# Both swiglus: blocks 4 to 11 of the second projection as seven products of quarters instead of eight

## The chip, the core and the metric

The kernel runs on one core of a Trainium2 chip. The metric is the device time of one execution in microseconds (us); TensorE is called PE here, VectorE DVE, ScalarE ACT, GpSimd POOL and SyncE SP. Before the change the median of three runs is 1713.47 us (1713.27 to 1714.15).

## The reference, cut to what matters

Two transformer layers and a third block of another kind run one after the other on 512 tokens of 1024 features, all in float32. The change touches the feed-forward part of the two layers, which stands after an attention and a layer norm in each:

```python
D_FF = 2816
def swiglu(x, w_in, w_out):
    gate, up = jnp.split(x @ w_in, 2, axis=-1)
    return (jax.nn.silu(gate) * up) @ w_out
x = layer_norm(DEEPNORM_ALPHA * x + swiglu(x, ffn_w_in[l], ffn_w_out[l]), ln_g[l, 1], ln_b[l, 1])   # l = 0, 1
```

The hidden activations have 2816 features, which are 22 blocks of 128. The third block ends in a feed-forward part too (`square(relu(f)) @ w_ff2`, 32 blocks), and its second projection is already computed in the way that the change brings to the swiglus.

## The kernel before, in words

**Numbers.** Each float32 operand is split into a high part, rounded to the type that PE multiplies (ACT writes it, `whi`, `hh`, `xh`), and the rest (DVE writes it, `wlo`, `hl`, `xl`). A product of two matrices then takes three matmuls (`mm3`).

**The swiglu stage.** `ffn` first computes blocks 0 to 3 plainly (`projections`). Blocks 4 to 21 are made by `pairs`: gate and up of one block form a pair, and their first projection is seven `product` steps of 12 matmuls of 256 columns each, with sums of the two weight tiles on DVE (`sums`, four instructions), copies out of PSUM on ACT (`keep`), sums on DVE (`combine`, `hidden`), silu on ACT (`gates`), and at last the hidden block (`hidden`), its high part on ACT and its low part on DVE (`hidden_low`).

**The second projection.** `rows` multiplies hidden blocks by rows of `ffn_w_out`, in groups of blocks (`FFN_GROUPS`: 4, 4, 4, 2, then 8 at the end). One piece is six matmuls of 512 columns: 128 tokens, two blocks, 512 output columns. Four blocks take 16 pieces, 4 split weight tiles and 8 additions from PSUM into `x` on DVE.

**The order.** All engines run through one list of steps (`Plan.steps`), each engine in that order and in order only. `PIECES` has a word of four digits for each iteration of `pairs`: how many pieces stand at four places between the products of that iteration. A split weight tile is a unit; `pump` puts its split so many units ahead of its use (`AHEAD_PAIRS` = 3). Eight slots hold split tiles.

**The seven products, as the last block has them.** For four hidden blocks at a time, `seven` takes the tokens, the hidden blocks and the output columns in halves and forms seven products of sums of quarters (`SEVEN`: a11, a12, s1, s4, s2, s3, a22), two pieces for each. `left_sum` forms the sums of hidden quarters on DVE, `left` splits each of the seven left operands (high part ACT, low part DVE), and the right operands are weight tiles to which an accumulating DMA from POOL's queue adds further tiles. A product is added to the output after each piece: nine of the 14 by DVE (`fadd`), five by ACT into `low_words` and then by an accumulating DMA from POOL's queue (`moved`, semaphores `added`). The raw hidden blocks lie in `hidden_words`, in the same memory as `hh`; `low_words` lies in the memory of `hl`.

Of the kernel before, what the change touches and what calls it, by code (L numbers as in the profile page):

```python
# [31 lines left out]
PIECES = "1011 1011 1011 1011 1011 1111 1111 1111 1111 1111 1111 1111 1111 1011 0101 0101 0101 0101 0000".split()  # L32
# [4 lines left out]
SEVEN_FIRST, SEVEN_LAST = 1, 6  # L37
# [8 lines left out]
PIECES = "1011 1011 1011 1011 1011 1111 1111 1111 1111 1111 1111 1111 1111 1011 0101 0101 0101 0101 0000".split()  # L46
# [27 lines left out]

class Piece:


    def __init__(self, u, unit, t, bank, start, before, value, tile, nh, sign, sent, earlier, after):
        self.u, self.unit, self.t, self.bank, self.start, self.before, self.value = u, unit, t, bank, start, before, value
        self.tile, self.nh, self.sign, self.sent, self.earlier, self.after = tile, nh, sign, sent, earlier, after  # L80
        self.moved = moved(tile, nh)


class Right:


    def __init__(self, buffer, need, sums=(), load=None):
# [3 lines left out]
class Pair:  # L91
# [8 lines left out]
    def __init__(self, kind, n, table, columns, blocks, first=None):  # L100
# [3 lines left out]
        self.first, self.seven = first, None if first is None or first // 4 > SEVEN_LAST else first // 4  # L104
# [35 lines left out]
class Plan:  # L140


    def __init__(self, kinds=None):
        self.steps, self.tiles, self.finished = [], [], {}
        self.units, self.kinds, self.summed = [], kinds, 0
# [8 lines left out]
        self.entry_of, self.entry_free = {}, {}  # L154
# [51 lines left out]
    def pump(self, most=2):  # L206

        while most and self.kinds and self.n_split < min(len(self.units) + self.ahead, len(self.kinds)):
# [7 lines left out]
            self.free_at.append(free)  # L216
            if SPLIT <= slot < SPLIT + EXTRA:
# [6 lines left out]
    def sum_next(self):  # L224

        n = self.n_split
        if n > self.summed and n < len(self.kinds) and self.kinds[n] == "s2":
            for i in range(3):
                self.prepare("sums", n + i)
            self.summed = n + 2  # L230
# [123 lines left out]
    def rows(self, kind, source, row0, nk, k_first=0, hh=True, norm=None, group=0):  # L354
# [14 lines left out]
        for word in order:  # L369
# [30 lines left out]
            if last:  # L400
                self.release(r.bank)
                self.step("rows_post", r)
                if kind == "f" and group == 0:
                    self.plain_rows = r.value
            self.relax(PACE[0])
# [117 lines left out]
    def seven(self, g):  # L523

        def ring(n):
            k = SEVEN_FIRST + n // 3
            return None if k > SEVEN_LAST else (n % 2 + 2, (4 * k + (2, 2, 0)[n % 3], (0, 1, 1)[n % 3]))

        first, last = 4 * g, 4 * g + 2
        turn, a = g - SEVEN_FIRST, g % 2  # L530
        needs = []
        for n in range(3):
            r = 3 * (g - SEVEN_FIRST) + n
# [3 lines left out]
        following = (a, (4 * g + 8, 0)) if g + 2 <= SEVEN_LAST else None  # L537
        landed = turn // 2 * 16 + 16
        rights = [Right(a, ("load", landed), [(a, "a", (first, 1))]), Right(b, ("load", b_need), (), b_next),
                  Right(a, ("a", 48 * turn + 16), [(a, "a", (last, 1))]),  # L540
                  Right(c, ("load", c_need), [(d, "d", (last, 1))], c_next),
                  Right(a, ("a", 48 * turn + 32), [(a, "a", (last, 0))]), Right(d, ("d", 16 * turn + 16), (), d_next),
                  Right(a, ("a", 48 * turn + 48), (), following)]
        rights[3].before = d_need
        if g == SEVEN_FIRST:
            self.paced = True
            self.left(1)
        for n, (name, chain, start, m, nh, sign) in enumerate(SEVEN):
            u = 7 * (g - SEVEN_FIRST) + n
            unit = self.unit("seven", rights[n], None)  # L550
            if g == SEVEN_LAST and n == 6:
                self.step("gain", self.fifth)
                self.step("unpark", unit)
            for t in range(2):
                if (chain, t) not in self.chains:
# [4 lines left out]
                piece = Piece(u, unit, t, bank, start, self.evicts.get(bank), value, tile, nh, sign, sent,  # L560
                              self.added.get((tile, nh)), after)
# [6 lines left out]
                if g == SEVEN_LAST and n == (3 if chain else 6):  # L568
                    self.release(bank)
                self.step("seven_post", piece)  # L570
                self.relax(PACE[0])
                if t == 1:
                    self.left(u + 2)
                self.flush()
                yield

# [7 lines left out]
    def left(self, u):  # L584

        g, n = SEVEN_FIRST + u // 7, u % 7
        if g > SEVEN_LAST:
# [13 lines left out]
        entry = (2, 3, 0, 1)[u % 4] if g < SEVEN_LAST else 2 + u % 2  # L601
# [13 lines left out]
    def product(self, pair, j):  # L615
# [24 lines left out]
        if j in (2, 7, 3):  # L640
            pair.combined[j] = self.count("combined") + 1
            self.read[{2: (1, 0), 7: (7, 0), 3: (6, pair.buf)}[j]] = pair.combined[j]
            if j != 3 and pair.kind == "relu":
                self.step("combine", pair, j, pair.clear)
            elif j != 3:
# [2119 lines left out]
```

## Time and profile before

| | |
|---|---|
| median of three runs | 1713.47 us |
| the profiled execution | 1713.66 us, its span 1711.9 us, granted PE clock 0.999 |
| matmuls | 10386 |
| PE busy | 1697.1 us |
| DVE busy | 1243.1 us |
| swiglu pairs | about 300 to 550 us and 900 to 1150 us of the span |
| seven products of the last block | about 1460 to 1670 us |

PE's busy time counts a matmul until its modelled end, so that it overlaps the next. The time that a matmul takes from the engine is the distance of two starts. The profiled execution lies 0.19 us above the median, and 1.8 us of it lie outside the span.

### The profile page before, as it was taken

To read this page: it belongs to the slowest core of one execution; us is meant where nothing else is said; L and a number is where in the kernel's file an instruction comes from. 1 tells how busy PE (TensorE), PEld (TensorE's weight loads), DVE (VectorE), ACT (ScalarE), POOL (GpSimd) and SP (SyncE) were. 2 spreads that over 40 slices of the span, in tenths; PEclk is the share of its full clock that TensorE was granted. 3 is DMA by queue.
4 is the path that set the end of the run, shared out by engine and by line. 5 is a ranking of instruction groups with operands and counts; after the bars stand their busy time and mean duration, and the time that the engine had idled before them with its cause. 6 is when DMAs were issued, how large, how long until landed. Compare 5 with 4: busy or idle time off the path is not lost.

```text
span 1711.9 us, 26482 instructions
## 1 busy us (share of the span) xinstructions
PE 1697.1 (99%) x10386; PEld 1480.7 (86%) x10386; DVE 1243.1 (73%) x2019; ACT 881.9 (52%) x1559; POOL 92.7 (5%) x157
## 2 busy tenths in 40 slices
PE   9999999999999999999999999999999999999998
PEld 7777788999999897777989999998988899899997
DVE  4588887777787745665877777868536686998897
ACT  4477744444444234665344444443546465766664
POOL 0222000000000000000000000000000000122121
PEclk9999999999999999999999999999999999999999
DMA  7343332333234332222233323343222335788875
GB/s 276 115 136 119 113 99 87 111 100 103 95 101 135 122 99 87 78 83 88 73 111 111 91 95 111 99 162 98 90 73 86 111 111 160 181 201 189 197 164 153
DMA packets 64559, 206.03 MB, mean 120 GB/s; under 512 B 8833, under 2 KB 9762, under 8 KB 64434
## 3 DMA queue, kind: packets, MB, share of 16 engines
q1 hardware_dynamic: 54610, 179.68, 32.5%
q0 software_dynamic: 9824, 24.65, 8.0%
q8 instruction: 83, 1.36, 0.3%
q14 instruction: 42, 0.34, 0.1%
HBM read 188.00 MB, written 9.48 MB: 115 GB/s over the span
## 4 chain that ended last, share of the span: by engine, by line
PE 94%; DVE 4%; ACT 1%; DMA 1%; issue 0%; SPq 0%; POOL 0%; DVEq 0%; ACTq 0%
PE ps L904 29%; PE ps L905 28%; PE ps L906 28%; PE ps L1319 1%; PE ps L1364 1%; PE ps L1390 1%; PE ps L1339 1%; PE ps L1378 1%; PE ps L1197 1%; DVE wlo L1965 0%; PE ps L1329 0%; DVE xl L2093 0%; DMA arena<-in_c_xt 0%; DVE small L2161 0%; DVE x L2157 0%
## 5 line engine op out<-in xcount | busy, mean ns | idle before, releaser
L1965 DVE TENSOR_TENSOR wlo<-raw,whi 128x1024 fp32r<-128x1024 f32 (+1 forms) x252 | 289.1, 1162 | 126.1 <-ACT whi L1551 125.8
L904 PE MATMUL ps<-xh,whi 128*128 128x256 f32 (+1 forms) x1016 | 331.7, 326 | 2.3 <-DVE xl L2093 2.3
L906 PE MATMUL ps<-xh,wlo 128*128 128x256 f32 (+1 forms) x1016 | 325.5, 320 | 0.0
L905 PE MATMUL ps<-xl,whi 128*128 128x256 f32 (+1 forms) x1016 | 325.2, 320 | 0.0
L1551 ACT ACTIVATE whi<-raw 128x1024 fp32r<-128x1024 f32 (+1 forms) x252 | 250.0, 1004 | 44.8 <-PE ps L906 27.6
L906 PE MATMUL ps<-whi,hl 128*128 128x512 f32 x604 | 235.4, 390 | 0.0
L904 PEld LDWEIGHTS ps<-xh,whi 128*128 128x128 f32 x1016 | 193.4, 190 | 25.9 <-issue 8.8
L904 PE MATMUL ps<-whi,hh 128*128 128x512 f32 x536 | 213.4, 398 | 0.7 <-DVE wlo L1965 0.6
L905 PE MATMUL ps<-wlo,hh 128*128 128x512 f32 x536 | 209.9, 392 | 0.0
L906 PEld LDWEIGHTS ps<-xh,wlo 128*128 128x128 f32 x1016 | 193.4, 190 | 14.4
L905 PEld LDWEIGHTS ps<-xl,whi 128*128 128x128 f32 x1016 | 193.6, 191 | 12.2
L904 PE MATMUL ps<-t_of,whi 128*128 128x256 f32 x624 | 176.0, 282 | 0.9 <-ACT stat L1559 0.9
L906 PE MATMUL ps<-t_of,wlo 128*128 128x256 f32 x624 | 176.6, 283 | 0.0
L905 PE MATMUL ps<-t_of,whi 128*128 128x256 f32 x624 | 176.5, 283 | 0.0
L906 PEld LDWEIGHTS ps<-whi,hl 128*128 128x128 f32 x604 | 113.4, 188 | 25.0
L904 PEld LDWEIGHTS ps<-t_of,whi 128*128 128x128 f32 x624 | 119.2, 191 | 7.2 <-ACT stat L1559 1.4
L905 PEld LDWEIGHTS ps<-t_of,whi 128*128 128x128 f32 x624 | 119.2, 191 | 5.3
L906 PEld LDWEIGHTS ps<-t_of,wlo 128*128 128x128 f32 x624 | 119.2, 191 | 0.0
L904 PEld LDWEIGHTS ps<-whi,hh 128*128 128x128 f32 x536 | 101.1, 189 | 20.6 <-issue 1.8
L904 PE MATMUL ps<-whi,xh 128*128 128x512 f32 x292 | 116.1, 398 | 1.0 <-DVE wlo L1923 0.6
L905 PEld LDWEIGHTS ps<-wlo,hh 128*128 128x128 f32 x536 | 101.1, 189 | 16.4 <-issue 0.2
L905 PE MATMUL ps<-wlo,xh 128*128 128x512 f32 x292 | 114.1, 391 | 0.0
(299 smaller groups left out, 3276.3 us busy)
## 6 DMA issues: line engine op xcount, KB each, us to landing
raw<-in_c_tiles SPq DMA_DIRECT2D x263, 512.0 KB, 3.7
x<-in_c_row_tiles SPq DMA_DIRECT2D x24, 512.0 KB, 5.6
x<-in_c_row_tiles POOLq DMA_DIRECT2D x24, 512.0 KB, 5.9
arena<-low_words POOLq DMA_DIRECT2D x30, 256.0 KB, 5.9
bias_skewed<-bias_rows SPq DMA_DIRECT2D x8, 640.0 KB
arena<-arena POOLq DMA_DIRECT2D x64, 64.0 KB, 3.5
arena<-bias_skewed SPq DMA_DIRECT2D x16, 256.0 KB, 4.1
x<-in_x SPq DMA_DIRECT2D x4, 512.0 KB, 5.8
```

What stands on the lines that cost most here:

```text
L904: e.matmul(o, ah, bh, start=start, stop=False, **more)
L905: e.matmul(o, ah, bl, start=False, stop=False, **more)
L906: return e.matmul(o, al, bh, start=False, stop=stop, **more)
L1197: m = e.transpose(ps[b][:, k * 128:k * 128 + 128], src[:, c:c + 128], ident[:])
L1319: e.matmul(ps[b][:, 0:n], q[c, i * 128:i * 128 + 128], k[c, 0:n], start=True, stop=True).then_inc(s.scores, 1)
L1339: m = e.matmul(ps[b][:, j * 128:512], self.V[:, j, h * 128:h * 128 + 128], self.aT[:, j, j * 128:512], start=(j == 0), stop=(j == 3))
L1364: m = e.matmul(ps[b][:, 0:n], q[c, queries], k[c, 0:n], start=turn == 0, stop=turn == 2)
L1378: m = e.transpose(ps[b][:, j * 128:j * 128 + 128], e_[:, j * 128:j * 128 + 128], ident[:])
L1390: m = e.matmul(ps[b][64 * a:64 * a + 64, j * 128:512], self.V_b[:, j, h * 64:h * 64 + 64], self.PT[a][:, j, j * 128:512], start=(j == 0), ...
L1551: e.activation(self.parts(m)[0][:, 0:n], src, ACT.Copy).then_inc(s.hi, 1)
L1965: e.tensor_tensor(lo[:, 0:n], src, f32(hi[:, 0:n]), ALU.subtract).then_inc(s.lo, 1)
```

## The change: what it does, and the diff

In both swiglus, hidden blocks 4 to 11 (groups 1 and 2) go through `seven` instead of `rows`; groups 0, 3 and 4 stay plain. The hidden product of these blocks is written raw to `hidden_words` and has no low part of its own. `seven`, `left` and their helpers take a `Stage`. The sums of products go to `x`. The right operands lie in the arena where two extra slots of split tiles were; these are closed at iteration 2 of `pairs` and opened again after it, and two small slots take the 512-column unit of each pair. `PIECES` has four pieces in each of the iterations 6 to 12; splits and sums are put off one by one (`SWIGLU_PACE`). The low parts of blocks 12 to 15 are written to the memory of `hl` that the moved products of group 1 pass through, and so wait for its accumulating DMAs; those of blocks 16 to 19 wait for group 2's.

```diff
-PIECES = "1011 1011 1011 1011 1011 1111 1111 1111 1111 1111 1111 1111 1111 1011 0101 0101 0101 0101 0000".split()
+PIECES = "1011 1011 1011 1011 1011 0010 1111 1111 1111 1111 1111 1111 1111 1101 0101 0101 0001 0000 0000".split()
+SWIGLU_AHEAD = 4
+CLOSE_AT, LOADS_FROM = 2, 3
+SWIGLU_PACE = 1, 1
+LEFT_AT = 5
+STAGES = [Stage(0, "ffn_w_out0", 1, 2, 0), Stage(1, "ffn_w_out1", 1, 2, 2), Stage(2, "w_ff2_2", 1, 6, 4)]
...
+        self.after = stage.base + stage.groups - (first % 8 >= 4) if first < 4 * stage.last + 12 else 0
...
 def pairs(self, pairs, pieces, places, ahead, first=(0, 0)):
         for i in range(len(pairs) + 1):
+            if i == LEFT_AT and self.stage.n < 2:
+                self.left(self.stage, 0)
+                self.left(self.stage, 1)
+            if i == CLOSE_AT and self.loads:
+                self.close_extra()
+            if i >= LOADS_FROM and self.loads:
+                self.step(*self.loads.pop(0))
...
-        rows = [self.rows("res", (f"ffn_w_out{layer}", 0), f0, nf, norm=norm if f0 == 14 else None, group=g)
+        rows = [self.seven(stage, g) if stage.covers(g) else
+                self.rows("res", (f"ffn_w_out{layer}", 0), f0, nf, norm=norm if f0 == 14 else None, group=g)
                 for g, (f0, nf) in enumerate(FFN_GROUPS)]
...
             elif what == "hidden":
+                elif pair.seven is not None:
+                    w.wait_ge(s.gates, pair.gates)
+                    w.wait_ge(self.events[free[0]], free[1])
+                    e.tensor_tensor(self.hidden_words[:, pair.blocks[0], :], first, second, ALU.mult).then_inc(s.combined, 1)
...
             elif what == "hidden_low":
                 for i, k in enumerate(pair.blocks):
-                    if pair.kind == "relu":
-                        for n in range(MOVED * (SEVEN_LAST - SEVEN_FIRST) - 4, MOVED * (SEVEN_LAST - SEVEN_FIRST)):
+                    if pair.after:
+                        for n in range(MOVED * pair.after - 4, MOVED * pair.after):
                             w.wait_ge(s.added[n % 4], 16 * (n // 4 + 1))
                     w.wait_ge(s.hh, pair.hidden[i] + 1)
                     e.tensor_tensor(self.hl[:, k, :], self.pair_out[pair.kind][i][pair.buf], f32(self.hh[:, k, :]),
```

**DVE, around the low part of block 12.** DVE's queue before, in the ninth of the 18 pairs of the first swiglu: the sum and the product that make the hidden block, a 512-column split of a weight tile, the low part of block 12 (it waits for its high part alone), the next split and the sums of the next pair.

```order
L2036 TENSOR_TENSOR arena<-arena,ps 128x256 [waits s_product]
L2047 TENSOR_TENSOR arena<-arena 128x512 [waits s_gates,s_combined]
L1965 TENSOR_TENSOR wlo<-raw,whi 128x512 [waits s_hi]
L2056 TENSOR_TENSOR hl<-arena,hh 128x512 [waits s_hh]
L1965 TENSOR_TENSOR wlo<-raw,whi 128x1024 [waits s_hi]
L1998 TENSOR_TENSOR arena<-stat,ps 128x256 [waits s_product,s_copied]
```

The same place in the changed kernel, from the same two rows on. L2103 is the low part of a left operand, L2134 the low part of block 12, L2039 a split, L2097 the addition of a product to `x`, L2082 a sum of hidden quarters.

```order
L2110 TENSOR_TENSOR arena<-arena,ps 128x256 [waits s_product]
L2125 TENSOR_TENSOR arena<-arena 128x512 [waits s_gates,s_combined]
L2059 TENSOR_TENSOR raw<-raw,arena 128x512 [waits s_sums,s_lo]
L2062 TENSOR_TENSOR raw<-raw 128x512
L2103 TENSOR_TENSOR xl<-hidden_words,xh 128x2x256 [waits s_left_hi]
L2134 TENSOR_TENSOR hl<-arena,hh 128x512 [waits s_added0,s_added3,s_hh,s_added2,s_added1]
L2039 TENSOR_TENSOR wlo<-arena,whi 128x1024 [waits s_hi]
L2039 TENSOR_TENSOR small_slots<-raw,small_slots 128x512 [waits s_hi]
L2097 TENSOR_TENSOR x<-x,ps 128x512 [waits s_rows]
```

The low part of block 12 now waits for the four semaphores of the accumulating DMAs, and splits, additions to `x` and sums stand behind it.

**DVE, a little further on.** Seven rows after the last of those stands this stretch: a split, the sums of the next pair, its hidden block, an addition to `x`, and the sums s2 and s4 of hidden quarters (L2084, L2086) with a left operand.

```order
L2039 TENSOR_TENSOR wlo<-arena,whi 128x1024 [waits s_hi]
L2053 TENSOR_TENSOR arena<-raw 128x512 [waits s_raw2,s_raw3,s_lo,s_sums]
L2055 TENSOR_TENSOR arena<-arena,raw 128x512 [waits s_sums]
L2110 TENSOR_TENSOR arena<-arena,ps 128x256 [waits s_product]
L2125 TENSOR_TENSOR arena<-arena 128x512 [waits s_gates,s_combined]
L2059 TENSOR_TENSOR raw<-raw,arena 128x512 [waits s_sums,s_lo]
L2097 TENSOR_TENSOR x<-x,ps 128x512 [waits s_fadd,s_rows]
L2062 TENSOR_TENSOR raw<-raw 128x512
L2084 SCALAR_TENSOR_TENSOR arena<-arena,hidden_words 128x512 [waits s_left_sum]
L2086 SCALAR_TENSOR_TENSOR hidden_words<-hidden_words,arena 128x2x256 [waits s_left_sum]
L2103 TENSOR_TENSOR xl<-hidden_words,xh 128x2x256 [waits s_left_hi]
L2134 TENSOR_TENSOR hl<-arena,hh 128x512 [waits s_hh]
```

The sixth row behind these is the split of the right operand of product s4 of group 2 (an L2039 row of 1024 columns). From the waiting low part to that split, both counted, there are 31 rows on DVE: 8 of 1024 columns, 19 of 512 and 4 of 256; before, a pair's rows were followed by those of the next pair and by the splits and additions of plain pieces alone.

**POOL.** Before, nothing of POOL's queue stood in the swiglus. Now the first group of seven has these rows (L2564 adds a weight tile to a right operand, L2573 adds a moved product to `x`), the last of which is the product that block 12's low part waits for:

```order
L2564 DMA arena<-in_c_row_tiles 128x1024 [waits s_lo] x2
L2564 DMA arena<-in_c_row_tiles 128x1024 [waits s_right2]
L2573 DMA x<-low_words 128x512 [waits s_res,s_evicted]
L2564 DMA arena<-in_c_row_tiles 128x1024 [waits s_lo]
L2573 DMA x<-low_words 128x512 [waits s_evicted]
L2573 DMA x<-low_words 128x512 [waits s_added1,s_evicted]
L2573 DMA x<-low_words 128x512 [waits s_added0,s_evicted]
L2564 DMA arena<-in_c_row_tiles 128x1024 [waits s_lo]
L2573 DMA x<-low_words 128x512 [waits s_evicted]
```

The last L2564 row serves group 2 already. So a group brings nine transfers of POOL's queue, four of 512 KB and five of 256 KB, where there were none.

## Rows read from the trace of the kernel before

**Rows 1.** The page: busy time of each engine, and the chain that ended last.

```profile
PE 1697.1 (99%) x10386; PEld 1480.7 (86%) x10386; DVE 1243.1 (73%) x2019; ACT 881.9 (52%) x1559; POOL 92.7 (5%) x157
...
PE 94%; DVE 4%; ACT 1%; DMA 1%; issue 0%; SPq 0%; POOL 0%; DVEq 0%; ACTq 0%
```

**Rows 2.** Windows: the swiglu's pairs (two windows), seven products of the last block.

```profile
core 0: us, PE busy (x) PEld busy (x) DVE busy (x) ACT busy (x) POOL busy (x), PEclk, DMA share, GB/s
...
342.40:385.20 42.80, 42.80 (x299) 39.96 (x298) 30.80 (x42) 19.47 (x32) 0.00 (x0) 1.00 0.33 100
...
470.80:513.60 42.80, 42.80 (x308) 40.45 (x308) 35.53 (x51) 19.60 (x33) 0.00 (x0) 1.00 0.35 101
...
1540.80:1583.60 42.80, 42.80 (x271) 38.70 (x271) 38.56 (x53) 28.36 (x46) 8.68 (x10) 1.00 0.83 190
```

**Rows 3.** PE's waits, 260 to 560 us: total, times, longest.

```profile
PE ps L904 <- ACT stat L1559: 0.5, 1, 0.5
PE ps L904 <- DVE wlo L1965: 0.3, 1, 0.3
```

**Rows 4.** Timeline, last block: a piece's last matmuls, product, moved product's way.

```profile
1611.13 0.40 PE L904 MATMUL ps<-whi,hl 128*128 128x512 f32 x1
1611.37 0.39 PE L905 MATMUL ps<-wlo,hl 128*128 128x512 f32 x1
1611.60 0.39 PE L906 MATMUL ps<-whi,hl 128*128 128x512 f32 x1
...
1611.82 0.28 PE L904 MATMUL ps<-t_of,whi 128*128 128x256 f32 x1
1611.94 0.28 PE L905 MATMUL ps<-t_of,whi 128*128 128x256 f32 x1
1612.02 0.60 ACT L1586 ACTIVATE low_words<-ps 128x512 f32<-128x512 f32 x1
...
1612.93 0.86 POOL L2491 DMA_DIRECT2D arena<-low_words  x1 [4.00 <-ACT low_words L1586]
```

**Rows 5.** Accumulating DMAs of `low_words`, issue to landing: that at 1612.93, all 21.

```profile
DMA to landing us min/median/max: 4.8/4.8/4.8
...
DMA to landing us min/median/max: 3.3/6.2/7.6
```

**Rows 6.** DVE's timeline in the last block (start, duration, idle time before it).

```profile
1560.72 0.41 DVE L1998 TENSOR_TENSOR arena<-stat,ps 128x256 f32<-128x256 f32 x1
1561.05 0.41 DVE L1998 TENSOR_TENSOR arena<-arena,ps 128x256 f32<-128x256 f32 x1
...
1570.13 0.68 DVE L1979 TENSOR_TENSOR arena<-raw 128x512 f32<-128x512 f32 x1
1570.85 0.69 DVE L1981 TENSOR_TENSOR arena<-arena,raw 128x512 f32<-128x512 f32 x1
1571.64 0.69 DVE L1985 TENSOR_TENSOR raw<-raw,arena 128x512 f32<-128x512 f32 x1
1572.26 0.68 DVE L1988 TENSOR_TENSOR raw<-raw 128x512 f32<-128x512 f32 x1
1572.86 1.22 DVE L1965 TENSOR_TENSOR wlo<-arena,whi 128x1024 fp32r<-128x1024 f32 x1
...
1579.34 0.68 DVE L2008 TENSOR_TENSOR arena<-hidden_words 128x512 f32<-128x512 f32 x1
1580.72 0.69 DVE L2029 TENSOR_TENSOR hl<-arena,hl 128x512 fp32r<-128x512 f32 x1 [0.70 <-ACT hl L1579]
1581.33 0.68 DVE L2023 TENSOR_TENSOR arena<-arena,ps 128x512 f32<-128x512 f32 x1
1581.93 1.22 DVE L1965 TENSOR_TENSOR wlo<-x,whi 128x1024 fp32r<-128x1024 f32 x1
1583.06 0.68 DVE L2023 TENSOR_TENSOR arena<-arena,ps 128x512 f32<-128x512 f32 x1
```

**Rows 7.** Groups of instructions by line, 342.4 to 470.8 us: count, busy us, mean ns.

```profile
L1610 ACT ACTIVATE hh<-arena 128x512 fp32r<-128x512 f32 x9 | 5.7, 632 | 27.0 <-DVE arena L2047 27.0
```

More of the change, by code:

```diff
@@ L72, in moved, with __init__, covers @@
     return tile % 2 == 1 and (tile, nh) != (1, 0)
+class Stage:
+    def __init__(self, n, table, first, last, base):
+        self.n, self.table, self.first, self.last, self.base = n, table, first, last, base
+        self.groups = last - first + 1
+    def covers(self, group):
+        return self.first <= group <= self.last
+STAGES = [Stage(0, "ffn_w_out0", 1, 2, 0), Stage(1, "ffn_w_out1", 1, 2, 2), Stage(2, "w_ff2_2", 1, 6, 4)]
 class Piece:
-    def __init__(self, u, unit, t, bank, start, before, value, tile, nh, sign, sent, earlier, after):
+    def __init__(self, stage, u, unit, t, bank, start, before, value, tile, nh, sign, sent, earlier, after, last, summed):
+        self.stage, self.last, self.summed = stage, last, summed
         self.u, self.unit, self.t, self.bank, self.start, self.before, self.value = u, unit, t, bank, start, before, value
@@ L582, in with_last, with left @@
                 yield
-    def left(self, u):
-        g, n = SEVEN_FIRST + u // 7, u % 7
-        if g > SEVEN_LAST:
+    def left(self, stage, at):
+        g, n, u = stage.first + at // 7, at % 7, 7 * stage.base + at
+        if g > stage.last:
             return
@@ L653, in product @@
             pair.gates = self.count("gates") + 1
[L654 removed]
+            self.step("gates", pair, pair.clear)
         if j == 3:
@@ L717, in ffn @@
         name = f"ffn_w_in{layer}"
-        self.pairs([Pair("swiglu", f, name, (FF + f * 128, f * 128), [f % 8]) for f in range(PLAIN, 22)], pieces, PIECES,
-                   AHEAD_PAIRS)
+        self.pairs([Pair("swiglu", f, name, (FF + f * 128, f * 128), [f % 8], f, stage) for f in range(PLAIN, 22)],
+                   pieces, PIECES, SWIGLU_AHEAD)
         assert next(pieces, None) is None
+        self.small = None
+        self.open_extra("rows", self.counts["rows"])
         self.ffn_blocks[layer] = self.counts["h"]
@@ L973 @@
 MOVED = 5
-FADD = (14 - MOVED) * (SEVEN_LAST - SEVEN_FIRST + 1)
+FADD = (14 - MOVED) * sum(stage.groups for stage in STAGES)
 LAST = len(FEED_GROUPS) - 1
@@ L2037, in vector @@
                                 ALU.add).then_inc(s.combined, 1)
-                if pair.seven is not None:
+                if pair.seven is not None and pair.kind == "relu":
                     continue
@@ L2156, in vector @@
                     w.wait_ge(s.x, 64)
+                    if r.added is not None and moved(t, nh):
+                        w.wait_ge(s.added[r.added % 4], 16 * (r.added // 4 + 1))
+                    elif r.added is not None:
+                        w.wait_ge(s.fadd, r.added)
                     e.scalar_tensor_tensor(x[:, t, c], x[:, t, c], 1.0 if r.group else ALPHA, ps[b][:],
```

211 lines of the change are left out of this document (127 added, 84 removed).

## The prediction

> **What bounds the kernel now.** I read the page first, then windows, then PE's waits, then single rows. The page has PE busy for 99% of the span, and 94% of the chain that ended last is PE's [rows 1]. Busy time alone doesn't prove that PE has no slack, so I looked at the swiglu's pairs: in both windows PE is busy for all of 42.80 us, DVE for 30.8 and 35.5 us and ACT for less than 20 [rows 2], and in 300 us around the first swiglu PE waits 0.8 us in all [rows 3]. So PE's own work sets the time there, matmul by matmul. What is to be seen beside it: in the last block's stretch of seven products PE is just as full, but DVE is at 38.6 of 42.8 us and the DMA engines at 0.83, against 0.33 to 0.35 in the swiglu [rows 2]. The form that the change brings is thus known to run without stalls, but close to DVE's limit, and there with seven pieces to a pair of blocks' products, not four.
>
> **What is removed.** A group of four blocks takes 16 pieces before and 14 after. Two groups in two swiglus: 8 pieces, 48 matmuls of 512 columns less (9476 rows of PE become 9428). Successive starts of such matmuls lie 0.23 us apart [rows 4]: 1611.13, 1611.37, 1611.60, and the next kind at 1611.82. A piece is 6 x 0.23 = 1.38 us. The gain is 48 x 0.23 = 11.0 us, 5.5 us in each swiglu, all of it on the path as long as PE stays full.
>
> **What is added, in DVE's time.** DVE's costs are distances of starts [rows 6]: 1024 columns 1.13 us (1581.93 to 1583.06), 512 columns 0.60 (1581.33 to 1581.93), 256 columns 0.33 (1560.72 to 1561.05). The four sums of a pair take 2.73 together (1570.13 to 1572.86), since two of them wait for the one before. A left operand behind a sum has to go to ACT and back: DVE idles 0.70 us (the row at 1580.72).
> - A plain group costs DVE four splits, eight additions and four low parts: 4 x 1.13 + 12 x 0.60 = 11.7 us.
> - A group of seven costs seven splits, nine additions, seven left low parts and four left sums: 7 x 1.13 + 20 x 0.60 = 19.9 us, and three of those 0.70 us of idling, 22.0.
> - A pair costs three splits of 1024, one of 512, the sums, three combinations and the hidden product: 3.4 + 0.6 + 2.7 + 1.0 + 0.7 = 8.4 us, 9.0 with a low part.
>
> PE's time for an iteration with four pieces: a product is 12 matmuls 0.12 us apart (1611.82, 1611.94 [rows 4]), 1.44 us; seven products and four pieces are 10.1 + 5.5 = 15.6 us. The 28 pieces of seven fill seven iterations, 109 us of PE. DVE has 7 x 9.0 less two low parts, and two groups: 61.8 + 44.0 = 106 us. Before, seven such iterations cost it about 63 + 1.75 x 11.7 less the low parts counted twice (4.2) = 79 us. So DVE goes from 73% to 97% in that stretch: it just fits if nothing stops it, and has 3 us to catch up in.
>
> **The wait that stops it.** DVE's row of block 12's low part waits for all accumulating DMAs of group 1, and it stands right behind that group's last piece (a22, moved). Its cover is gone by construction, so I price the whole path from the end of that piece's last matmul on PE. In the last block, eviction starts 0.20 us after it (1611.82 to 1612.02), lasts 0.60, and POOL's transfer starts 1.11 us after PE's end (1612.93) [rows 4]; this very kind, the last of a group, landed after 4.8 us [rows 5]. That makes 5.9 us. In the swiglu ACT first has to make the high part of block 12, which waits for DVE's product of the same pair: 0.6 us more [rows 7]. I take **6.5 us** from the end of the piece until DVE goes on. The ends are 3.3 us of landing and no copy ahead (4.4 us) and 7.6 us of landing with it (9.3) [rows 5]. What is queued behind it on DVE: 31 rows, itself among them, until the split for product s4 of group 2 is done. They cost 8 x 1.13 + 19 x 0.60 + 4 x 0.33 = 21.8 us, plus 0.3 inside the sums, 0.2 for two other dependent rows, 1.4 for two left operands behind sums and 0.4 where a split follows a left operand at once (ACT makes the one high part after the other): 24.1 us. PE can start that product when it is done: 6.5 + 24.1 = 30.6 us after the end of the piece. By its own work PE wants it after 12 products and 6 pieces, 17.3 + 8.3 = 25.6 us. So PE loses **5.0 us**. An earlier point on the same path: the split for a12 is seven rows on (3 x 1.13, 3 x 0.60, 0.33 with the waiting row), ready at 12.0 us; PE wants it after 5 products and 2 pieces, at 10.0. Those 2 us are part of the 5. After s4 DVE has 15.1 us of rows for 15.7 us of PE until the split for s3, so the loss is not made up and hardly grows.
>
> The same wait stands once more, at block 16, for group 2. There it lies four steps of PE later: a product, a piece, two products and a piece behind the last moved piece, 7.1 us, when the DMA has landed (6.5): nothing. At its upper end, 9.3, it would hold DVE for 2.2 us, but the iterations behind have two pieces or one, where PE needs 12.9 us and DVE about 10.8: nothing.
>
> **What lies beside other work.** ACT gets three more splits, three more left high parts and five evictions a group, less than 7 us on an engine that is busy for under half of the stretch [rows 2]. Eight slots become six big and two small ones; each split waits for a product that PE has passed by one to four steps, and SP's row tiles and the two gain vectors behind the pairs are wanted over 10 us later. The DMA engines carry, besides what they carried, four accumulated weight tiles and five moved products, 3.25 MB per group over 3.5 iterations, 55 us; the last block has the same in two iterations of seven pieces, 40 us, and PE stays full [rows 2]. All these at nothing; if ACT or a weight tile came late, the price would be part of the slower rival's.
>
> **The sum.** Against the profiled execution (1713.66 us, of which the span is 1711.9): 1713.66 - 11.0 + 2 x 5.0 = 1712.7; the median of the runs is 0.19 lower: **1712.5 us**. The gain and the new wait nearly cancel.
>
> A rule against the row on the transfer: the Trainium skill, "DMA: Bandwidth & Descriptors", section "Anatomy of one DMA", puts a transfer of POOL's queue at about 2.0 us plus its bytes by 436 GB/s, which is 2.6 us for 256 KB. The 21 rows here show 3.3 at the least and 6.2 in the middle, among other transfers and with an addition at the destination, so I don't go by it. By the rule DVE would go on after 4.3 us, PE would lose 2.8 us a swiglu, and the sum would be 1708.1 us, a time of the first rival's.
>
> **The rivals.**
> - *The wait is there but shorter, or PE has more ahead than I count.* For it: DMA engines in the swiglu are far less loaded (0.33 before) than in the last block (0.83) [rows 2], and the shortest landing was 3.3 us [rows 5]. With that landing and the copy ahead DVE goes on at 5.0 us, PE loses 3.5 us a swiglu: 1709.5. Against it: the 4.8 us row is already a transfer with few others beside it, and POOL adds 512 KB for the next a11 just ahead of this one. Chance 0.16, with times of 1706 to 1710.
> - *The wait never reaches PE.* All 11.0 us stay: 1702.5. It needs DVE to do the 31 rows 5 us faster, or the low part to be waited for elsewhere. The last block, where PE is full beside such work, speaks for it, but there this wait comes long after its transfers. Chance 0.14, up to 1706.
> - *DVE becomes the bound of the whole stretch (the other side).* Place: iterations 6 to 12. My 106 us of DVE are 3 us under PE's 109. Every high part that ACT has only just made costs DVE idle time that isn't in the distances; if rows cost 5% more than I count, DVE needs 111 us, so 2 to 3 us are lost before the wait and 1.2 more on the 31 rows: about 4 us a swiglu on top of the 5. 1712.5 + 8 = 1720.5. It decides from 3% on: below that the slack takes it. A landing of 7.6 us alone [rows 5], 2.8 us later, would give 1718.1. Against it: the last block's 38.6 of 42.8 us, where rows and idling counted in the same way give 22.0 + 2 x 7.7 = 37.4 of 39.5 us, 95%, and PE is full. Chance 0.24, times of 1717 to 1723.
>
> **How the numbers follow.** My forecast, gain and wait within some 2 us a swiglu of each other, has 0.46, and times of 1709.5 to 1716.5. A measurement of this kernel tells about 0.2%, 3.4 us, from no change: faster means below 1710.0, slower above 1716.9. Faster: the first rival, the second, and the low edge of the forecast, 0.15 + 0.14 + 0.03 = 0.32. Slower: the third but for its low edge and a little of the forecast, 0.24. Within: 0.44. The range leaves out most of the second rival and the upper part of the third: 1705.5 to 1718.5.
>
> **What would show each step right or wrong.** PE: 48 matmuls less, starts still 0.23 and 0.12 us apart. DVE's low-part row of block 12 (L2134) waiting some 4 to 5 us for a DMA, once in each swiglu, and nothing at block 16. PE idle time of about 2 us before the a12 product and 3 us before the s4 product of group 2, released by splits or additions of DVE; DVE without gaps for 24 us behind its wait; windows of the stretch with DVE near 41 of 42.8 us. PE waits spread over group 1 as well would mean the third rival; none at all, the second. The prediction is wrong if PE's waits in the two swiglus sum to less than 7 or more than 14 us, or if outside the swiglus anything moves: there the order is the same.

## The result, and the profile after

| | before | after |
|---|---|---|
| median of seven runs | 1714.15 us | 1718.75 us |
| lowest and highest | 1713.27 to 1715.56 us | 1718.23 to 1720.44 us |
| granted clock, profiled execution | 0.999 | 0.996 |
| profiled execution and its span | 1713.66 and 1711.9 us | 1718.85 and 1717.1 us |

The ratio is 1.0027, with a 95% interval of 1.0016 to 1.0039: 4.6 us slower, where I had forecast 1 us faster. 1718.75 us lies just above the range, and the likeliest case was not the one that came.

The page of the kernel after, its busy times:

```profile
PE 1692.5 (99%) x10338; PEld 1477.2 (86%) x10338; DVE 1271.0 (74%) x2063; ACT 908.5 (53%) x1603; POOL 124.8 (7%) x193
```

Against [rows 1] the 48 matmuls are gone and DVE has 28 us more. PE's idle time is the span less its busy time: 14.8 us before, 24.6 us after. That is 9.8 us more, and I had said 10.0. The two figures agree in part by luck: 2.3 us of the idle time is a wait for ACT that I had not forecast. And the time is 6.2 us above the sum of 1712.7 for the profiled execution.

PE's waits after, the first swiglu from 430 us (two rows) and then the second from 1020 us (total, times, longest):

```profile
PE ps L970 <- DVE wlo L2039: 3.5, 2, 2.0
PE ps L970 <- ACT stat L1632: 1.6, 1, 1.6
...
PE ps L970 <- DVE wlo L2039: 4.7, 3, 2.1
```

To compare with [rows 3]: the waits for splits of DVE are the new ones, some 2 us each. The wait for the copy by ACT was 0.5 us and is 1.6 us now, in both swiglus. In the second one the three waits for splits are 1.94, 0.62 and 2.11 us long and end at 1031.95, 1047.01 and 1050.81.

The timeline after, around block 12's low part (start, duration, what; in brackets the idle time before it and what ended it). The last moved piece of group 1 ends on PE at 427.40:

```profile
428.75 0.63 ACT L1684 ACTIVATE hh<-arena 128x512 fp32r<-128x512 f32 x1 [3.29 <-DVE arena L2125]
...
429.29 0.58 ACT L1659 ACTIVATE low_words<-ps 128x512 f32<-128x512 f32 x1
...
430.16 0.86 POOL L2573 DMA_DIRECT2D x<-low_words  x1 [2.72 <-ACT low_words L1659]
...
430.42 0.69 DVE L2103 TENSOR_TENSOR xl<-hidden_words,xh 128x512 fp32r<-128x512 f32 x1 [0.56 <-ACT xh L1652]
...
433.79 0.69 DVE L2134 TENSOR_TENSOR hl<-arena,hh 128x512 fp32r<-128x512 f32 x1 [2.68 <-DMA x<-low_words]
...
439.48 0.50 PE L970 MATMUL ps<-whi,xh 128*128 128x512 f32 x1 [1.97 <-DVE wlo L2039]
...
458.33 0.50 PE L970 MATMUL ps<-whi,xh 128*128 128x512 f32 x1 [1.48 <-DVE wlo L2039]
```

This is the whole path of the prediction, and nothing of the kind stands at block 16. ACT makes the high part of block 12 first, then the eviction, POOL issues, the transfer takes 3.4 us, and DVE goes on 6.4 us after the piece's end (433.79 - 427.40). The a12 product starts 12.1 us after it and the s4 product of group 2 30.9 us after it.

What stands in no step of the prediction is in the windows after. The granted clock is the third number from the end of a row:

```profile
440.00:441.00 1.00, 1.00 (x4) 0.73 (x4) 0.95 (x2) 0.01 (x1) 0.00 (x0) 0.70 0.78 229
441.00:442.00 1.00, 1.00 (x5) 0.88 (x4) 0.35 (x1) 1.00 (x3) 0.00 (x0) 0.50 1.02 348
442.00:443.00 1.00, 1.00 (x7) 1.00 (x6) 0.47 (x2) 1.00 (x2) 0.00 (x0) 0.50 0.81 320
443.00:444.00 1.00, 1.00 (x7) 1.00 (x7) 1.00 (x1) 0.78 (x1) 0.00 (x0) 0.60 0.23 86
...
1052.00:1053.00 1.00, 1.00 (x3) 0.79 (x3) 0.83 (x1) 0.00 (x0) 0.00 (x0) 0.50 1.03 252
...
1384.00:1385.00 1.00, 1.00 (x7) 1.00 (x6) 0.96 (x3) 1.00 (x2) 0.00 (x0) 0.50 0.66 135
```

Three times while PE has work its clock falls from 2.4 GHz (1.00) to 1.2 GHz (0.50); a fourth fall, behind its last matmul, stands in the kernel before as well and costs nothing. Summed over the windows, the first fall takes 0.30 + 0.50 + 0.50 + 0.40 = 1.7 us of PE, and the other two are as long. PE is busy all the while, so these microseconds are in no wait. Each fall begins 0.6 to 1.6 us after PE has been idle for some 2 us: 1.97 us before 439.48, 2.11 before 1050.81, and 1.84 before 1380.92, in the norm ahead of the last block. Not every such idle time has a fall behind it: that of 1.94 us before 1031.95 has none. The third fall is not the change's own. The kernel before has the norm's idle time too (1.83 us); its profile has no fall there, but C1 below, which is the kernel before under another name, has one (a row of its timeline, and a window):

```profile
1376.72 0.38 PE L907 MATMUL ps<-xh,whi 128*128 128x256 f32 x1 [1.84 <-DVE xl L2099]
...
1378.00:1379.00 1.00, 1.00 (x6) 1.00 (x6) 1.00 (x2) 0.97 (x5) 0.00 (x0) 0.50 0.00 0
```

The end of the pairs, after; the last wait of PE for a copy by ACT:

```profile
546.64 0.63 ACT L1684 ACTIVATE hh<-arena 128x512 fp32r<-128x512 f32 x1 [2.35 <-DVE arena L2125]
547.18 1.04 ACT L1624 ACTIVATE whi<-raw 128x1024 fp32r<-128x1024 f32 x1
548.13 0.36 ACT L1632 ACTIVATE stat<-ps 128x256 f32<-128x256 f32 x1
...
548.54 0.39 PE L970 MATMUL ps<-t_of,whi 128*128 128x256 f32 x1 [1.61 <-ACT stat L1632]
```

In the changed kernel splits are put off one by one, and ACT makes the high part of one of the last splits (1.04 us, at 547.18) ahead of the copy that PE waits for. Before, the copy had no split in front of it, and PE waited 0.47 us, the 0.5 of [rows 3].

### The profile page after: what moved, and what is told of

Its sections match the earlier page's. It is cut to its first block, busy times and chain, and to the rows that moved or that the text cites. A ratio compares the mean times of both kernels' runs of the same rounds, so it can differ in the third digit from the quotient of the medians.

```text
span 1717.1 us, 26557 instructions
## 1 busy us (share of the span) xinstructions
PE 1692.5 (99%) x10338; PEld 1477.2 (86%) x10338; DVE 1271.0 (74%) x2063; ACT 908.5 (53%) x1603; POOL 124.8 (7%) x193
## 3 DMA queue, kind: packets, MB, share of 16 engines
q0 software_dynamic: 15008, 38.28, 12.5%
## 4 chain that ended last, share of the span: by engine, by line
PE 89%; DVE 6%; ACT 1%; issue 1%; DMA 1%; POOL 0%; SPq 0%; DVEq 0%; ACTq 0%
PE ps L970 28%; PE ps L971 27%; PE ps L972 27%; DVE wlo L2039 2%; PE ps L1392 1%; PE ps L1437 1%; PE ps L1463 1%; PE ps L1412 1%; PE ps L1451 1%; PE ps L1270 1%; ACT whi L1624 1%; DMA arena<-arena 1%; DVE x L2097 0%; DVE xl L2171 0%; DMA arena<-in_c_xt 0%
## 5 line engine op out<-in xcount | busy, mean ns | idle before, releaser
L2039 DVE TENSOR_TENSOR wlo<-raw,whi 128x1024 fp32r<-128x1024 f32 x236 | 285.4, 1221 | 120.4 <-ACT whi L1624 120.1
L1624 ACT ACTIVATE whi<-raw 128x1024 fp32r<-128x1024 f32 x236 | 245.9, 1051 | 47.1 <-PE ps L972 31.0
L970 PE MATMUL ps<-t_of,whi 128*128 128x256 f32 x768 | 217.8, 284 | 3.8 <-ACT stat L1632 3.2
L971 PE MATMUL ps<-t_of,whi 128*128 128x256 f32 x768 | 218.1, 284 | 0.0
L972 PE MATMUL ps<-t_of,wlo 128*128 128x256 f32 x768 | 218.0, 284 | 0.0
L971 PEld LDWEIGHTS ps<-xl,whi 128*128 128x128 f32 x1048 | 200.5, 191 | 12.1
L970 PE MATMUL ps<-whi,hh 128*128 128x512 f32 x424 | 168.7, 398 | 0.0
L971 PE MATMUL ps<-wlo,hh 128*128 128x512 f32 x424 | 165.8, 391 | 0.0
L970 PE MATMUL ps<-whi,xh 128*128 128x512 f32 x380 | 151.5, 399 | 8.1 <-DVE wlo L2039 7.5
L970 PEld LDWEIGHTS ps<-t_of,whi 128*128 128x128 f32 x768 | 147.7, 192 | 11.4 <-ACT stat L1632 3.6
L971 PEld LDWEIGHTS ps<-t_of,whi 128*128 128x128 f32 x768 | 147.7, 192 | 6.1
L972 PE MATMUL ps<-whi,xl 128*128 128x512 f32 x380 | 148.8, 392 | 0.0
L2039 DVE TENSOR_TENSOR wlo<-arena,whi 128x1024 fp32r<-128x1024 f32 x75 | 91.5, 1220 | 11.1 <-ACT whi L1624 11.1
```

What stands on the lines that cost most here:

```text
L970: e.matmul(o, ah, bh, start=start, stop=False, **more)
L971: e.matmul(o, ah, bl, start=False, stop=False, **more)
L972: return e.matmul(o, al, bh, start=False, stop=stop, **more)
L1624: e.activation(self.parts(m)[0][:, 0:n], src, ACT.Copy).then_inc(s.hi, 1)
L2039: e.tensor_tensor(lo[:, 0:n], src, f32(hi[:, 0:n]), ALU.subtract).then_inc(s.lo, 1)
```

## The experiments

The runs of the kernel before beside them have medians of 1714.1 to 1715.1 us. E1 to E3 and B ran on one chip, E4, E5 and C1 on a second, E6 and C2 on a third.

The table has, from the profiled execution of each, the time from the first to the last row of a product in the pairs of each swiglu, and the falls of the clock while PE had work left. C1 and the kernel before agree in both stretches to 0.01 us, so that differences here are clearer than those of medians.

| | median, us | pairs of the first swiglu | of the second | falls of the clock in the swiglus / in the norm |
|---|---|---|---|---|
| before | 1714.15 | 260.18 | 260.19 | 0 / 0 |
| after | 1718.75 | 261.04 | 262.51 | 2 / 1 |
| E1 | 1712.72 | 258.25 | 258.25 | 0 / 1 |
| E2 | 1712.58 | 259.43 | 259.45 | 2 / 0 |
| E3 | 1709.69 | 258.33 | 258.33 | 2 / 0 |
| B | 1716.11 | 260.63 | 260.41 | 0 / 0 |
| E4 | 1713.43 | 259.59 | 259.83 | 2 / 0 |
| E5 | 1732.89 | 269.74 | 269.83 | 4 / 0 |
| E6 | 1705.08 | 255.14 | 255.13 | 0 / 0 |
| C1 | 1715.05 | 260.19 | 260.19 | 0 / 1 |
| C2 | 1737.07 | 270.95 | 271.73 | 2 / 0 |

**E1: block 12's low part waits less.** The moved products of group 1 go to other places, so that each of blocks 12 to 15 waits for the transfer out of its own place alone, which for block 12 is an early one.

```diff
     def evict_to(self, p):
+        if p.stage.n < 2 and not p.last:
+            return self.low_words[:, (p.sent - MOVED * p.stage.base + 3) % 4 + 4, :]
...
-                        for n in range(MOVED * pair.after - 4, MOVED * pair.after):
+                        sents = range(MOVED * pair.after - 4, MOVED * pair.after)
+                        if pair.kind == "swiglu" and pair.first < 16:
+                            sents = sents[pair.first - 12:pair.first - 11]
+                        for n in sents:
```

> The changed kernel, but in the swiglus the last moved product of group 1 passes through the memory of block 15's low part instead of block 12's, and the low parts of blocks 12 to 15 each wait only for the one moved product that used their own place. Theory (wait and clock): in the changed kernel DVE's wait for the DMA costs PE 3.5 us of waiting in the first swiglu and 4.7 in the second, and the granted clock falls after each of the two waits of about 2 us, 1.7 us of PE's time each; so 10 to 12 us go: 1707 to 1709 us, the wait rows for splits are gone, and the granted clock is 1.00 through both swiglus. Rival (DVE is the bound of the stretch anyway, its rows 97% of PE's time): PE waits of 2 us or more a swiglu stay at other splits, 1711 us or more. Rival (the clock falls by itself, not after waits): dips of the same number remain, 1710 us.

Measured: 1712.72 us (1709.26 to 1714.38, 11 runs), ratio 0.9984 (0.9975 to 0.9992), 6.0 us below the kernel after; I had expected 10 to 12. DVE's timeline and PE's waits of it:

```profile
430.38 0.68 DVE L2139 TENSOR_TENSOR hl<-arena,hh 128x512 fp32r<-128x512 f32 x1
...
PE ps L970 <- DVE wlo L2041: 4.2, 2, 2.1
PE ps L970 <- ACT stat L1634: 3.2, 2, 1.6
...
454.90 0.50 PE L970 MATMUL ps<-whi,xh 128*128 128x512 f32 x1 [2.11 <-DVE wlo L2041]
```

The low part has no idle time ahead of it. The last moved piece of group 1 ends at 426.76 in this execution, so the low part stands 3.6 us behind it, against 6.4 in the kernel after, and the s4 product 28.1 us, against 30.9: both 2.8 us earlier. The wait at a12 is gone. The one at s4 is not: 2.1 us. So DVE is late there by itself. With the low part's wait the first swiglu lost 1.97 + 1.7 (the fall) + 1.48 = 5.15 us, without it 2.11: the wait costs some 3 of the 5 us, and DVE's own work the other two. The runs also show the clock's price: three runs at 1.000 took 1709.3 to 1710.0 us, four at 0.997 1712.8 to 1714.4. The changed kernel's runs don't sort so: at 0.998 they took 1718.5 and 1718.8 us and at 0.996 1718.7 to 1720.4. A fall ahead of a wait for DVE can lower the clock at no cost, as the first one there does: from the low part to s4 it is 24.54 us in the first swiglu, with a fall between, and 24.54 in the second, without one.

**E2: the copy ahead of the split.** At the end of the pairs no split is planned at two places, so that ACT's copies come first.

```diff
     def product(self, pair, j):
...
+        if pair.kind == "swiglu" and (pair.first, j) in ((20, 3), (21, 5)):
+            return
         if not self.by_hand:
             self.pump(PUMP)
```

> The changed kernel, but the last split of a weight tile within the pairs is put behind the copy of the last pair's product 7 instead of ahead of it on ACT. Theory: PE waits 1.6 + 0.2 us there in each swiglu (0.5 before the change), because ACT makes that split's high part first; now 0.5 again, 1.3 us a swiglu less: 1716.1 us. Rival: the wait only moves to the rows behind, whose split is now later: 1718.7 us.

Measured: 1712.58 us (1711.52 to 1716.76, 11 runs), ratio 0.9994 (0.9985 to 1.0003). PE's waits for the copy fall from 3.2 to 1.3 us:

```profile
PE ps L972 <- ACT stat L1634: 1.3, 2, 0.7
```

I had expected 1716.1 us; it came 3.5 us lower, and the copy doesn't account for that. The two profiled executions lie 7.1 us apart. The stretch ahead of the first swiglu, where the edit changes nothing, was 0.95 us shorter, and the norm's fall is missing, 1.5 us. The pairs are 1.6 us shorter in the first swiglu, where the copy's wait fell by 1.0 and a small one of 0.2 us behind it is gone, and 3.1 us in the second. There the clock fell too, but at 1030 us, ahead of the wait at s4, and not at 1051, behind it, where it costs its full 1.7 us. So the edit itself is worth some 1.2 us a swiglu, and the rest is where the clock fell.

**E3: both edits.**

> Both edits together. Theory: the gains add, 1704.5 to 1706.5 us: the 11.0 us of the 48 matmuls, less the PE waits that are left (about 1 us a swiglu) and a clock dip of 1.7 us at the norm before the last block. Rival (DVE the bound): 1708.5 us or more, with PE waits in the stretch of seven products.

Measured: 1709.69 us (1708.26 to 1711.5, 8 runs), ratio 0.9971 (0.9961 to 0.9981). I had expected 1704.5 to 1706.5 us; this is the time of the rival, DVE as the bound. The median is 3.0 us below E1's. The profiles can't confirm that as the worth of the second edit: the pairs are as long as E1's (258.33 and 258.25 us), since what the copy gives back a fall takes in each swiglu. One wait at s4 is left in each, and here the clock falls behind it:

```profile
454.64 0.80 PE L972 MATMUL ps<-whi,xh 128*128 128x512 f32 x1 [2.12 <-DVE wlo L2043]
455.24 0.63 PE L973 MATMUL ps<-wlo,xh 128*128 128x512 f32 x1
455.66 0.63 PE L974 MATMUL ps<-whi,xl 128*128 128x512 f32 x1
456.09 0.63 PE L972 MATMUL ps<-whi,xh 128*128 128x512 f32 x1
```

Starts lie 0.43 us apart, against 0.23 in [rows 4]. In E1 an idle time of 2.11 us at the same place was followed by none of this.

**B: the slots alone.** The kernel before, with the six big and two small slots of the changed one and four units of splits ahead, and no seven products in the swiglus.

```diff
+            if i == 2 and pairs[0].kind != "relu":
+                self.close_extra()
...
+        self.small = [(SPLIT + EXTRA + i, ("t_lo", 4 * layer + 4)) for i in range(2)]
...
-                   AHEAD_PAIRS)
+                   4)
+        self.small = None
+        self.open_extra("rows", self.counts["rows"])
```

> The kernel before, with only the change's handling of split tiles in the swiglus: two extra slots closed from iteration 2 on, two small slots, four units ahead, and the gain vectors loaded after the last pair's small unit. No seven products, the old pattern of pieces. Theory: at nothing, as the prediction had it, 1714.1 us within 1. Rival: six slots are too few and 2 us or more of the 4.6 us that the change lost are theirs: 1716 us or more.

Measured: 1716.11 us (1714.34 to 1716.98, 11 runs), ratio 1.0007 (0.9998 to 1.0017), clock 0.998 to 1.000. That is 1.6 us above the kernel before beside it and just above the 1716 us from which I had said that the slots cost 2 us or more, but the interval takes in both no cost and 2.9 us. Its profile says less: the pairs are 0.4 and 0.2 us longer, with neither a fall nor the long wait at the end. So the slots cost some 0.7 us in the swiglus; whether they cost more is open.

**E4: three pieces a unit.** E3, with one piece less in each of the iterations 8, 9 and 10.

```diff
-PIECES = "1011 1011 1011 1011 1011 0010 1111 1111 1111 1111 1111 1111 1111 1101 0101 0101 0001 0000 0000".split()
+PIECES = "1011 1011 1011 1011 1011 0010 1111 1111 1101 1101 1101 1111 1111 1111 0111 1101 0001 0000 0000".split()
```

> The kernel of e3, with the table of places changed: three pieces instead of four in the iterations 8, 9 and 10 of each swiglu, the three that are put off go to iterations 13, 14 and 15. e3's trace still has one wait of PE of 2.1 us in each swiglu, for the split of s4 of group 2, and DVE is busy almost without a gap in the 30 us before it. Theory (DVE's work is the bound there, and PE's idle time of 2 us also brings the granted clock down to half for some 3.4 us, which costs 1.7 us more): by the rows, a unit of two pieces takes 3.6 us of DVE and 2.8 us of PE, so that three pieces put off give DVE 5.4 us against 4.2 us of PE, and the wait shrinks by about 1.2 us to below 1 us in each swiglu; with the clock no longer falling there, the time is 2 x 1.2 + up to 2 x 1.7 us below e3's 1709.7, 1704 to 1707 us, and the granted clock of its runs 0.999 to 1.000. Rival (the wait is one of order: the split of s4 stands too late in DVE's queue for its product, whatever DVE has to do): the wait stays at 2 us and the time at 1709 to 1710 us.

Measured: 1713.43 us (1711.24 to 1714.61, 11 runs), ratio 0.999 (0.9981 to 0.9999): slower than E3, where I had expected 1704 to 1707. The wait at s4 did shrink, from 2.1 to 0.5 us, but a new one came 34 us later. Its timeline, DVE and then PE:

```profile
489.81 0.68 DVE L2063 TENSOR_TENSOR raw<-raw,arena 128x512 f32<-128x512 f32 x1
495.54 0.69 DVE L2141 TENSOR_TENSOR hl<-arena,hh 128x512 fp32r<-128x512 f32 x1 [5.04 <-DMA x<-low_words]
...
498.03 0.39 PE L972 MATMUL ps<-t_of,whi 128*128 128x256 f32 x1 [2.70 <-DVE wlo L2043]
```

It is block 16's low part, waiting for group 2's last moved product: the wait that the prediction priced at nothing, because it lay 7.1 us of PE behind that product. The pieces put off had used up this distance. PE waited 2.7 us for it in the first swiglu and 2.9 in the second, and the clock fell behind both.

**E5: splits five units ahead instead of four**, on E3 (`SWIGLU_AHEAD = 5`), to see whether the wait at s4 is one of order.

> The kernel of e3, with the splits of the weight tiles planned five units ahead of PE in the swiglus instead of four. If the wait for the split of s4 is one of order, it stands earlier in DVE's queue by about a unit and the wait of 2.1 us goes: 1702 to 1706 us. If DVE's work is the bound, the place in the queue changes nothing of the sum of the work, the wait stays near 2 us or moves to a left operand, and the time stays within 1 us of e3's 1709.7 us; with six slots in a ring, a split further ahead may wait for its slot instead, which gives 1710 to 1713 us.

Measured: 1732.89 us (1731.35 to 1733.38, 4 runs), ratio 1.0105 (1.0092 to 1.0119). The wait at s4 stays, 2.26 us, so an earlier place in the queue doesn't help it. The large loss is elsewhere and its place was not expected: early in the pairs PE waits 6.34 us in the first swiglu for a copy by ACT, and 6.7 in the second. ACT itself stood 11.71 us for the transfer of a weight tile whose high part was planned ahead of the copy. Why that transfer comes so late stays open.

```profile
368.89 1.06 ACT L1628 ACTIVATE whi<-raw 128x1024 fp32r<-128x1024 f32 x1 [11.71 <-DMA raw<-in_c_tiles]
...
370.36 0.55 PE L972 MATMUL ps<-t_of,whi 128*128 128x256 f32 x1 [6.34 <-ACT arena L1636]
```

**E6: E4, with E1's edit for blocks 16 to 19 as well.**

```diff
+        if p.stage.n < 2:
+            return self.low_words[:, (p.sent - MOVED * p.stage.base + 2) % 4, :]
...
-                        if pair.kind == "swiglu" and pair.first < 16:
-                            sents = sents[pair.first - 12:pair.first - 11]
+                        if pair.kind == "swiglu":
+                            sents = sents[pair.first % 4:pair.first % 4 + 1]
```

> The kernel of e4, and besides blocks 16 to 19 get what e1 gave blocks 12 to 15: the moved products of group 2 are put into the memory of hl in an order in which its last one lies where block 19 will, and the low part of each of these blocks waits for the transfer out of its own place alone. In e4 the wait at s4 had shrunk from 2.1 to 0.5 us as the theory of DVE's work says, but 34 us later PE waited 2.7 us, since DVE stood 5.04 us for a transfer before the low part of block 16. Theory (the pieces that were put off had moved group 2's last moved product up to block 16's low part, the same wait as block 12's at another place): DVE's 5.04 us and PE's 2.7 us go in both swiglus, and with them the fall of the clock behind them; the time is 5.4 us and up to 3.4 us below e4's 1713.4, 1704.5 to 1708 us, and below e3's 1709.7. Rival (four pieces in iteration 13 and three in 14 and 15 are themselves too much there): a wait near 498 us of 1 us and more stays, 1709 to 1713 us.

Measured: 1705.08 us (1703.75 to 1705.3, 5 runs), ratio 0.994 (0.9927 to 0.9952), as expected: the fastest version, 10 us below the kernel before. The window around the wait, first of E4 and then of E6:

```profile
480.00:498.00 18.00, 15.32 (x106) 13.95 (x104) 12.47 (x19) 8.82 (x15) 1.72 (x2) 1.00 0.50 124
```

```profile
480.00:498.00 18.00, 18.00 (x130) 16.97 (x130) 17.09 (x25) 9.74 (x16) 1.72 (x2) 1.00 0.67 177
```

PE's 2.7 us of waiting are gone, and DVE does 17.1 us of work there instead of 12.5. In the whole of the two swiglus only waits of 0.7 us or less are left, the clock doesn't fall, and the pairs of each are 5.05 us shorter than in the kernel before, of a forecast gain of 5.5.

**C1 and C2: what an idle time costs beside its length.** The kernel before, with waits of PE for a DVE sum in four iterations of each swiglu.

```diff
+            if j == 7:
+                self.last_seventh = pair.combined[7]
+            if j == 2:
+                pair.force = self.last_seventh if pair.kind == "swiglu" and pair.number in FORCED else 0
...
+                if j == 2 and pair.force:
+                    w.wait_ge(s.combined, pair.force)
```

> The kernel before, with eight waits of PE added and nothing else: in four iterations of each swiglu, PE's next product waits until DVE has combined the product just ended, so that PE idles for the length of a copy on ACT and a sum on DVE, by the rows about 1.3 us if both are free and up to 2.5 us if DVE is in a split. It asks what an idle time costs beside its own length. Theory (the granted clock falls after PE has idled about 2 us amid dense work): the trace shows stretches of matmul starts 0.43 us apart instead of 0.23 us and windows of granted clock 0.5 right after the idle times near 2 us, each some 3.4 us long and worth 1.7 us, and the time is the sum of the idle times plus 1.7 us for each fall: with eight idle times of 1.5 us and four falls 1714.5 + 12 + 7 = 1733 us. Rival (the falls in the changed kernel have another cause): clock 0.999 to 1.000 as in the kernel before, and the time grows by the idle times alone, 1726 us.

C1's condition named a field that is empty in this kernel, so it added no wait. What it measured is the kernel before against itself, and that it has a fall in the norm in some executions: 1715.05 against 1714.12 us, ratio 1.0002 (0.9993 to 1.0011).

> What c1 was to do: its waits did not come into the program, so that it was the kernel before under another name (1715.05 against 1714.12 us, clock 0.998 to 1.000). Now the kernel before with four waits of PE in each swiglu, each for the DVE sum of the product that has just ended. Theory (the granted clock falls when PE idles some 2 us amid dense work): idle times of 1.3 us to 2.5 us at the eight places, and stretches of matmul starts 0.43 us apart for some 3.4 us behind those near 2 us, each worth 1.7 us; the runs' clock is 0.994 to 0.997, and the time is 1714.5 plus the sum of the idle times plus 1.7 us for each fall: with eight idle times of 1.5 us and four falls 1733 us. Rival (the falls in the changed kernel came from something else in it, such as its transfers): clock 0.999 to 1.000, the time grows by the idle times alone, 1726 us.

Measured: 1737.07 us (1735.6 to 1737.42, 4 runs), ratio 1.0127 (1.0112 to 1.0143). PE's waits for the sum, then two of the eight in its timeline, and two windows:

```profile
PE ps L909 <- DVE arena L2006: 16.6, 8, 4.4
...
361.71 0.39 PE L909 MATMUL ps<-xh,whi 128*128 128x256 f32 x1 [1.49 <-DVE arena L2006]
413.17 0.58 PE L909 MATMUL ps<-xh,extra 128*128 128x256 f32 x1 [4.40 <-DVE arena L2006]
...
362.00:363.00 1.00, 1.00 (x10) 1.00 (x10) 0.00 (x0) 0.00 (x0) 0.00 (x0) 1.00 0.37 98
...
414.00:415.00 1.00, 1.00 (x6) 1.00 (x6) 0.00 (x0) 0.00 (x0) 0.00 (x0) 0.50 0.89 266
```

None of the six idle times of 0.9 to 1.5 us had a fall behind it. Both of the 4.40 us had one: PE worked at 1.2 GHz for 3.3 us after the first and for 5 us after the second, which costs 1.6 and 2.5 us. With the 16.6 us of waits that makes 20.7 of the 22.0 us lost. The rest is the overlap that an idle time leaves out: ahead of the row at 361.71 the starts lie 1.77 us apart instead of 0.12, so that this idle time of 1.49 us costs 1.65, and 0.16 more at each of eight places is 1.3 us. My numbers were off (four falls, 12 us of idling), the mechanism was not: nothing but idle time was added, and the clock fell.

## Why the prediction was wrong, point by point

- **The gain, 48 x 0.23 = 11.0 us:** right. 10338 matmuls instead of 10386, same distances at full clock.
- **DVE resumes 6.5 us after the piece:** right in the sum (6.4) by luck. POOL started the transfer 2.8 us after the piece's end and not 1.7, since the eviction stood further back behind block 12's high part, and the transfer landed in 3.4 us and not in 4.8.
- **12.0 and 30.6 us, PE loses 2 and 3:** right as a total (12.1 and 30.9; 5.15 us with the fall inside). But I read all of it as the low part's wait. E1 shows that 2.1 us are DVE's own lateness: it reaches that row 3.6 us behind the piece's end without the wait (426.76 to 430.38), and PE can start s4 24.5 us later, 28.1 us after the end of the piece, for a product that it wants after 25.6. The 24.1 us were right; their start without the wait was not zero. "Needs the low part to be waited for elsewhere" was therefore too little for the second rival, and the third rival (DVE the bound) was true for one place of the stretch, at 2 us instead of 4.
- **Block 16 at nothing:** right here, and E4 shows how near it lay.
- **"All these at nothing":** this step failed, for ACT at the end of the pairs. I checked that slots and splits come early enough for their products, not what ACT does between PE's products when the splits are put off: 1.1 us a swiglu, 2.3 in all. I had named a late ACT as part of the slower rival, but gave it no price.
- **No term for the clock:** this step failed too. I counted idle time of PE at its length. Three falls in the profile took 1.7 us each. The first lay ahead of s4's wait, which it shortened, and cost nothing; that at 1052 us cost in full and is the change's. That at 1383 us cost 1.5 us against a profile before that has none, but it belongs to the norm's own idle time, and C1 has it without the change.
- **"Wrong if outside the swiglus anything moves":** by that sign the prediction was wrong, for the norm's fall moved. Its other sign, the waits in the two swiglus, came out inside, at 5.3 + 6.5 = 11.8 us.

The two profiled executions, stretch by stretch, from PE's rows:

| stretch | before, us | after, us | difference |
|---|---|---|---|
| from the start to the first swiglu's pairs | 290.38 | 290.84 | +0.5 |
| pairs of the first swiglu | 260.18 | 261.04 | +0.9 |
| from there to the second swiglu's pairs | 331.46 | 331.48 | 0.0 |
| pairs of the second swiglu | 260.19 | 262.51 | +2.3 |
| from there through the norm's idle time | 235.07 | 235.05 | 0.0 |
| from there to the end of PE's last matmul | 328.59 | 330.13 | +1.5 |

That is the 5.2 us between 1713.66 and 1718.85. The two swiglus, which I had at -1.0 us, came out at +3.2: the 11.0 us gained, 10.2 us more of waits (5.3 and 6.5 us against 0.8 and 0.8 [rows 3]) and 1.7 us for each of two falls make +2.6, and the overlap that C2 shows, 0.16 us at each of five waits more, 3.4. Of the 6.2 us by which the sum was short, then, the copy is 2.3, the fall behind s4 1.7, the norm's fall 1.5, and 0.5 us were lost ahead of the first swiglu, where both kernels do the same. That is 6.0, and the overlap covers the small rest. The forecast wait itself was right within half a us: 3.5 + 0.2 us of waits and the fall's 1.7, less the 0.3 that was there before, make 5.1 in the first swiglu, and 4.7 + 0.2 - 0.3 = 4.6 in the second, against 5.0 each. The measured median lies 0.25 us above the range; without either of the two terms that I had at nothing it would lie inside.

That the waits cause the falls in the swiglus is shown from two sides: C2 adds nothing but idle time and brings them, and E6, without the waits, has none. Why one idle time of 2 us is followed by a fall and the next is not stays open.

## What to carry to other kernels

A new wait of the bounding engine has two prices: its length, and what the clock does afterwards; with idle times of 2 us and more, count both, but the second only where no later wait for another engine takes it up. When two waits come on one path, take one away in thought and ask where the engine stands then: the next limit may be a microsecond behind it. And a wait for "all transfers of a group" is worth splitting by place: here E1's and E6's edits were a few lines and, with E2's two splits put off and a thinner pattern of pieces, turned 4.6 us lost into 10 us won.

## What the runs showed of the hardware

- In the eleven profiles the granted clock fell to 0.50 seventeen times while PE had work left, for 3.4 us or twice that. Each fall began during an idle time of PE of 1.83 us or more, or within 1.6 us of its end. Idle times of 2.25 us and more were followed by a fall all eight times (E4, E5, C2), those of 1.83 to 2.12 us in 9 of 20 cases, and those of 0.8 to 1.6 us never.
- The idle time of 1.83 or 1.84 us in the norm, in the same program, had a fall behind it in one execution (C1) and not in another (the kernel before); over all kernels in 3 of 11 profiles.
- E1's runs differ by it: at clock 1.000 they took 1709.3 to 1710.0 us, at 0.997 up to 1714.4.
- An accumulating transfer of 256 KB from POOL's queue landed in 3.4 us behind block 12's piece, and the ten of the first swiglu had a median of 3.6 us, at the lower end of the 3.3 to 7.6 us of [rows 5].
